# Attention probabilities of two layers: divided by their sums on VectorE before the transposes, or on TensorE and the output after them

## The reference, cut to what matters

```
def one_block(qi):
    s = jnp.einsum('bqgrd,bkgd->bgrqk', qi, k).astype(jnp.float32) * scale
    p = jax.nn.softmax(s, axis=-1).astype(v.dtype)
    return jnp.einsum('bgrqk,bkgv->bqgrv', p, v)
...
y = jnp.concatenate([o_mla, o_gqa, o_conv], axis=-1) * jax.nn.silu(p[..., OFF_GATE:])
x_new = x + gate[:, None, :] * (y @ w_out)
```

## Time and profile before

| | |
|---|---|
| median of 3 runs | 2105.72 us (2103.67 to 2107.43) |
| profiled execution | 2100.2 us, of which the span is 2098.3 us |
| busy share of the span | PE 97%, PEld 77%, DVE 75%, ACT 59%, POOL 1% |
| attention of layer 0 | about 206 to 295 us of the span |
| attention of layer 1 | about 455 to 519 us of the span |
| longest line of the last chain | PE L759, 84% |

### The profile page before, as it was taken

One profiled execution on the slowest core, in us unless ns is written; L12 is line 12 of the kernel. 1 busy time (PEld: TensorE's weight loads), 2 busy tenths in 40 slices (PEclk: granted clock), 3 DMA queues, 4 the chain that ended last, 5 costly groups with the idle time before them and its releaser, 6 DMA issues.

```text
span 2098.3 us, 28488 instructions
## 1 busy us (share of the span) xinstructions
PE 2030.1 (97%) x10909; PEld 1623.5 (77%) x10909; DVE 1569.5 (75%) x1892; ACT 1236.5 (59%) x1411; POOL 30.2 (1%) x29
## 2 busy tenths in 40 slices
PE   6999998999899989999999999999999999999998
PEld 4785577866688467888878888888888888888887
DVE  4862756856744577675579898988989898898987
ACT  3233544454431555554447777777777777777775
POOL 1000000000000000000000000000000000000000
PEclk8999999999999999999999999999999999999998
DMA  9202522255732855467699999999999999999991
GB/s 328 93 26 98 200 81 71 98 194 189 259 121 81 313 195 215 173 205 186 222 349 339 374 354 373 344 380 366 358 373 350 374 344 380 366 361 372 349 373 55
DMA packets 261037, 539.47 MB, mean 257 GB/s; under 512 B 6170, under 2 KB 41649, under 8 KB 260828
## 3 DMA queue, kind: packets, MB, share of 16 engines
q1 hardware_dynamic: 258352, 530.71, 70.2%
q0 software_dynamic: 1856, 5.39, 0.7%
q10 hardware_dynamic: 748, 2.24, 0.3%
HBM read 536.22 MB, written 2.10 MB: 257 GB/s over the span
## 4 chain that ended last, share of the span: by engine, by line
PE 89%; DVE 5%; DMA 3%; ACT 2%; issue 1%; SPq 0%; PEldq 0%; DVEq 0%
PE bank L759 84%; PE bank L797 2%; PE bank L1398 1%; DMA ring<-in_w_mod 1%; DVE ring_r L2106 1%; DMA ring<-in_attn_w_qkv 1%; PE bank L868 1%; DVE nmax L2143 1%; DMA ring<-in_ada_w 1%; PE bank L829 1%; ACT ring_r L1585 1%; PE bank L1072 0%; DVE H L2026 0%; DVE H_r L2035 0%; DMA ring<-in_ff_w 0%
## 5 line engine op out<-in xcount | busy, mean ns | idle before, releaser
L759 PE MATMUL bank<-H_r,scratch_r 128*128 128x512 f32 x1664 | 573.5, 397 | 0.8 <-DVE H_r L2046 0.5
L759 PE MATMUL bank<-scratch_r 128*128 128x512 f32 x1472 | 420.6, 390 | 0.0
L759 PEld LDWEIGHTS bank<-H_r,scratch_r 128*128 128x128 f32 x1664 | 313.3, 189 | 67.2 <-DVE H_r L2046 2.2
L759 PEld LDWEIGHTS bank<-scratch_r 128*128 128x128 f32 x1472 | 276.2, 188 | 58.2
L2548 DVE TENSOR_TENSOR ring_r<-ring,H_r 128x2048 fp32r<-128x2048 f32 x128 | 292.4, 2289 | 28.6 <-ACT H_r L1877 25.9
L759 PE MATMUL bank<-H_r,ring_r 128*128 128x256 f32 (+2 forms) x1296 | 303.5, 316 | 1.4 <-ACT H_r L1496 1.4
L1877 ACT ACTIVATE H_r<-ring 128x2048 fp32r<-128x2048 f32 x128 | 245.9, 1921 | 95.1 <-PE bank L759 95.1
L759 PE MATMUL bank<-scratch_r,ring_r 128*128 128x256 f32 (+2 forms) x1280 | 278.6, 345 | 6.5 <-ACT scratch_r L1569 2.1
L759 PE MATMUL bank<-H_r,modrow_r 128*128 128x512 f32 x672 | 262.4, 390 | 0.0
L759 PE MATMUL bank<-ring_r,scratch_r 128*128 128x512 f32 x896 | 248.1, 391 | 0.0
L759 PEld LDWEIGHTS bank<-scratch_r,ring_r 128*128 128x128 f32 (+1 forms) x1280 | 217.4, 196 | 36.5 <-issue 4.9
(11 more groups left out here) (246 smaller groups left out, 2316.7 us busy)
## 6 DMA issues: line engine op xcount, KB each, us to landing
ring<-in_moe_w SPq DMA_DIRECT2D x96, 2048.0 KB, 8.6
scratch<-in_moe_w SPq DMA_DIRECT2D x73, 2048.0 KB, 8.4
ring<-in_ada_w SPq DMA_DIRECT2D x24, 2048.0 KB, 9.7
ring<-in_ff_w SPq DMA_DIRECT2D x14, 2048.0 KB, 7.7
ring<-in_w_mod SPq DMA_DIRECT2D x12, 2048.0 KB, 11.6
ring<-in_ff_w SPq DMA_DIRECT2D x8, 1792.0 KB, 8.4
ring<-in_w_in SPq DMA_DIRECT2D x6, 2048.0 KB, 8.4
ring<-in_attn_w_qkv SPq DMA_DIRECT2D x6, 2048.0 KB, 8.5
```

The costliest lines, as they stand in the source:

```text
L759: m = nc.tensor.matmul(out_, w, x_, start=first, stop=last)
```

## The change

TensorE no longer spreads the reciprocals. VectorE's scale(s-1) takes the reciprocals, waits for them, and multiplies both heads' probabilities in `PR` by them in place. `prob_ready` is raised after the second product, and TensorE waits for it in front of the transposes instead of in front of the values. The multiplication of `GATE` by the spread reciprocals is gone. The waits for the score banks in front of the transposes are gone too, since `prob_ready` is behind them.

```diff
@@ -1059,19 +1059,13 @@
                     elif what == "transposes":
 
                         copy_turns[u] = []
+                        pe.wait_ge(prob_ready, 24 * l + u + 1)
                         for i in range(2):
-                            sb_, sn = score_turns[u][i]
-                            pe.wait_ge(bank_taken[sb_], sn + 1)
                             copy_turns[u].append((t.g % 8, t.g // 8))
                             transposes(lambda bk: [(bk[:, P * k:P * k + P], PR[:, u % 2, i, P * k:P * k + P], P)
                                                    for k in range(nk)])
                     else:
                         b, _ = start()
-                        pe.wait_ge(prob_ready, 24 * l + u + 1)
-                        for i in range(2):
-                            nc.tensor.matmul(bank[b][64 * i:64 * i + 64, P:2 * P],
-                                             rinv[:, u % 4, i:i + 1].broadcast_to([P, 64]), ident,
-                                             start=True, stop=True)
                         for rb, rn in copy_turns[u]:
                             pe.wait_ge(bank_taken[rb], rn + 1)
                         for k in range(nk):
@@ -2261,7 +2255,11 @@
                     elif what == "scale":
                         b, n = score_turns[u][1]
                         dve.wait_ge(bank_taken[b], n + 1)
-                        v.reciprocal(rinv[:, u % 4, :], rsum[:, u % 2, :]).then_inc(prob_ready, 1)
+                        link(v.reciprocal(rinv[:, u % 4, :], rsum[:, u % 2, :]))
+                        for i in range(2):
+                            last = v.tensor_scalar(PR[:, u % 2, i, 0:keys], PR[:, u % 2, i, 0:keys],
+                                                   rinv[:, u % 4, i:i + 1], None, ALU.mult)
+                        last.then_inc(prob_ready, 1)
                     elif what == "transposes":
                         nk = keys // P
                         b, n = ready()
@@ -2271,7 +2269,6 @@
                     elif what == "values":
                         b, n = ready()
                         q = slice(LAT * stream + P * qt, LAT * stream + P * qt + P)
-                        link(v.tensor_tensor(GATE[:, pair, q], bank[b][:, P:2 * P], GATE[:, pair, q], ALU.mult))
                         v.tensor_tensor(GATE[:, pair, q], bank[b][:, 0:P], GATE[:, pair, q], ALU.mult)\
                             .then_inc(bank_taken[b], 1)
                         if mixed:
```

## The result

The changed kernel took 2122.84 us, the median of 4 runs (2119.37 to 2124.13). The kernel before took 2104.69 in runs beside them (4 runs, 2098.31 to 2107.43). The ratio is 1.0087, with a 95% interval of 1.0064 to 1.0109: 18 us slower. The forecast was 2111.6 with a range up to 2120, so the sign was right, the size was three times the forecast's 5.9, and the time lies above the range. The profiled execution took 2124.13 us, of which the span is 2121.2.

The account below looks back on a forecast made before the run. TensorE was taken to bound both attention stages, with VectorE taking over in layer 0's GQA half. Layer 0 at +3.1 and layer 1 at +2.8 gave +5.9 us on the median 2105.7: 2111.6 us, range 2102 to 2120.

Parts of the forecast that it names:

- GQA of layer 0: Four units there gain nothing: VectorE at 10.8 us takes the place of TensorE at 10.7.
- T(0): Start of TensorE's transposes of unit 0 (number = unit): 465.4 instead of 462.8 in layer 1, 216.4 instead of 213.4 in layer 0.
- The marches: Start times worked out step by step through each layer's attention: layer 1 ends 2.8 us later, layer 0 3.1.
- S(5): Scores of unit 5 in layer 1, behind the late start: 5.1 us late.
- rival (c): TensorE's clock falls in the starts' waits, 3 us more per layer: 2114.6 to 2117.6 us; chance 0.16.
- The spreading: Thirty-six spreadings leave TensorE at 0.37 us each, 13.3 us if nothing else becomes late.
- MLA of layer 0: TensorE saves 1.5 us per four units; 0.7 is left; its three fours win 0.7, 0.7 and 0.1.
- The loop over three engines: Layer 0's MLA half: TensorE, ScalarE, VectorE take 5.0 us over two steps against TensorE's 4.3, once in four units.
- VectorE's busy time: Over the 36 units it rises by 21 us: products of both widths added, 36 x 0.29 removed.
- (a): TensorE stays the bound everywhere and all 36 spreadings count: 2092.4 us; chance 0.08.
- (d): VectorE's products take 0.68 us instead of 0.486, in some 20 units: 2119.6 us; chance 0.06.
- (b): Only the first wait of each layer is lost, the late start mostly absorbed: +1.8 us, 2107.5 us; chance 0.24.

Follow-up runs that it names:

- e8: The change in all 12 units of layer 1 and none of layer 0, otherwise the kernel before: 2116.58 us, ratio 1.0056.
- e6: The kernel before, its spreading kept and nothing scaled, with each unit's transposes waiting for its reciprocals: 2114.66 us, ratio 1.0044.
- e9: The change in both layers from unit 4 on, units 0 to 3 as in the kernel before: 2106.4 us, ratio 1.0018.
- e1: The changed kernel with idle TensorE products filling the waits of units 0 to 2 in each layer: 2112.79 us, ratio 1.0041.
- e10: e6 with idle TensorE products, two ahead of the waits for units 0 and 1, one for unit 2, both layers: 2111.71 us, ratio 1.0035.
- e2: The changed kernel with VectorE scaling the unit before ahead of the rope in steps 1 to 3 of each layer: 2113.37 us, ratio 1.0048.
- e3: The kernel before without the spreading and its multiplication on VectorE, attention left undivided by its sums: 2098.85 us, ratio 0.9969.
- e4: The kernel before with two unread VectorE products added behind each reciprocal, TensorE waiting for none: 2108.88 us, ratio 1.0030.

## Why the prediction was wrong in size

By its own steps, with what the runs showed:

- **The sign and the place** were right. GQA of layer 0 and both starts bear the loss, T(0) and T(1) wait for VectorE's product, and VectorE stands in the chain there. e8 shows one start per layer, e6 that the wait makes most of it. The starts alone do not: e9 has no late start and still loses 1.76 in layer 0's GQA units.
- **The marches** held. With the clock held, in e1, and the layer's own offset taken off, T(0), T(1) and T(2) of layer 1 start at 465.5, 470.7 and 476.0, where the march had 465.4, 470.7 and 475.95; S(5) is 5.3 late, where it had 5.1, and T(6) of layer 0 5.1, where it had 4.7. In the changed kernel itself the sign that was named, T(2) of layer 1 5 to 6 us late with VectorE's product as releaser, did not come: it is 9.4 late and stands behind TensorE's own slow products.
- **The step that failed: the clock.** The sum has TensorE's work "of fixed length", and the fall of the clock stands beside it as rival (c), with a chance of 0.16 and 3 us per layer. It was what happened. The price was near (3.8 and 3.6 us per layer, e1), the chance was not. The prediction weighed it by one stretch of the third attention, 694 to 698, in which TensorE was busy for 1.91 of 4 us at full clock, and did not ask how thin the work around its own three waits was. The row of the same group with the clock at 0.50 spoke for the fall, and the march had already worked out the waits of 3.0, 2.6 and 1.0. The clock fell where work came in bursts between gaps (changed, e6), and held when the gaps were filled (e1, e10). The Trainium skill ("TensorE: Matmul & The Clock Gate", Why this matters for your kernels) warns of idle gaps between bursts, and these four runs agree with it in kind. The gaps that its row names are longer than the waits of e2 and e6, of 2.00 us at most, behind which the clock fell too; here the measurement decides. Rival (c)'s own time ended at 2117.6, because the terms below were missing in it too.
- **The spreading was worth 0.22, not 0.37** (e3, and the 3.82 per unit of layer 1). The prediction took the length of a removed group as its worth, without asking what of the work behind it would come into the open. In layer 1 this makes -1.3 of -2.2. (The loss of 0.2 at its end is there: behind the two waits of 0.50 the output product is later by 0.15 to 0.4 than the last exps.)
- **MLA of layer 0 won 0.4, not 1.5.** From T(10) to T(22) it took 40.20 us, where it took 40.56 before (the table's -0.08 begins at unit 7 and has a loss of the last GQA units in it). The loop over three engines is there as drawn, once in four units. The forecast left 0.7 of the 1.5 that TensorE saves in four units. TensorE saves only 4 x 0.22 = 0.88, and the loop takes 0.64 of it (T(10) to T(14) is 11.80 in e3 and 12.44 in the changed kernel), where the forecast took 0.8. It is the same mis-sized term again. That VectorE's products take the gain, and not the missing spreading, is shown by e3, which wins 2.6 from T(10) to T(22).
- **The sum mended**: starts 5.15 + 5.33, clock 3.8 + 3.6, the rests -0.1 - 1.3: 16.5 us, which is the changed kernel's own row. It lies inside the interval of the ratio (1.0064 is 13.5 us) and is 1.7 short of the difference of the medians.
- **VectorE's busy time** rose by 16.3, not by 21. The forecast took 31.7 for what is added (24 x 0.97 + 12 x 0.70). The 72 products are 31.6 long one by one, as forecast, but an instruction that starts before the end of the one in front is busy time only once: a pair of 0.48 each counts 0.88, and the 72 count 28.6. The multiplication that went was 36 x 0.288 = 10.4. That leaves 18.2, and the overlap of each pair with what follows it takes off more; how much was not added up.

Rivals (a), TensorE the bound everywhere, and (d), slow products, fell: the products took 0.484 in the median (256 keys 0.351), as the row of the same form said. By the table of the Trainium skill ("VectorE: DVE Perf Modes", section on the TRN2 errata) the product of 512 would be 0.33 us; this trace does not agree. (b) fell too: nothing of the late start was absorbed. In e6 and e10 it came through 1:1 to the end of each attention.

What stays open: how much of the difference lies past the attention. From the third attention to the end, profiles of these kernels differ by some us with no pattern that follows the edits (the stretch from its last exps to the end of the feed-forward stage took 302.8 us before, 306.0 after, 301.7 in e1, 306.2 in e10). The ratios of e8 and e9 stand for 4 and 3 us more than their sums, e6's for 2 less; one profile each can't settle whether that is such variation.

## What to carry to other kernels

Where a wait is added at the start of a stage, in which TensorE has small work, price it twice: once as waiting, and once as TensorE's work behind it at half clock, until well past the last wait (in layer 0 the waits ended at 223 and the clock came back at about 232). In this kernel the second was 7.4 of the 16.5 us lost in attention. Where TensorE's late result feeds the engine that it waits for, each lengthens the other. A removed group of matmuls is worth the change of the period of the loop it was in, which one run without it shows (0.22), and not its own length (0.37). And an order written out by hand fits the dependencies it was written for: a new dependency on the last instruction of a step makes everything ahead of it in the queue, here a rope of 2 us, part of the path.

## What was not expected of the hardware

- Idle work on TensorE shortened the kernel. Seven and six idle 128x512 products of 0.95 us each (2.84 for three) in the waits of the two layers kept the granted clock at 1.00 and won about 7 us in two layers, with nothing else changed.
- The clock fell behind waits of 0.76 and 1.84 us (e2), and of 2.00 and 1.14 us (e6), amid transposes and products of 32 rows. It fell in e4 too, where no wait was longer than 1.00 us. In e9 TensorE waited 1.54 us and was busy for 2.79, 2.46 and 3.55 of 4 us from 222 to 234, and the clock stayed at 1.00. The length of a wait alone did not tell which it would be.
- Pieces at 0.50 were not all twice as long: the rope's product went from 1.04 to 1.91, the scores' four from 1.13 to 2.08, T(1) from 1.09 to 1.97.
- Taking away four small matmuls (0.37) lengthened what stands behind them by 0.15, in the middle of layer 1 in each of the three kernels whose chain was read for it (changed, e3, e9).
